# Merging two of three 256-column matmuls of a weight tile into one of 512 columns, and moving sixteen modulation rows

## The chip, the cores and the metric

One NeuronCore of a Trainium2 chip runs the kernel as one program. The metric is the device time of one execution in microseconds, as a median over several runs.

## The reference

Two transformer-like blocks over 256 tokens of width 2048, batch 1, in float32. What matters here is that nearly all of the work is a chain of matrix products with large weights:

```python
mod = (c_act @ ada_w + ada_b)            # 6 x 2048 modulation values
h = rmsnorm(x, norm1_g) * (1 + sc1) + sh1
z = h @ w_in                             # q, k, v, gates, lx, ly, ga, gb
o_a = nsa_attention(...); o_b = gelu(ly) * rg_lru(u, ...)
merged = sigmoid(ga) * (o_a @ proj_a) + sigmoid(gb) * (o_b @ proj_b)
x = x + g1 * (merged @ w_out)
h = rmsnorm(x, norm2_g) * (1 + sc2) + sh2
gate, val = split(h @ w_up)              # 2 x 6144 columns
x = x + g2 * ((gelu(causal_dwconv(gate)) * val) @ w_down)
```

A second block (sliding-window attention, a state-space mixer, a gated output) follows; the change leaves it as it is.

## The kernel before

Activations lie transposed in SBUF: 128 partitions of features by 256 tokens. Each product is made at better than one pass of the reduced float32 type: every weight and every activation is held as a high half (rounded) and a low half (the rest), and a weight tile (128x128 at one k) takes three matmuls with 256 moving columns, high by high, high by low and low by high (`terms` in `unit`, line 1792). Each matmul instruction loads its weights itself. `put_pair` lays the low half of an activation behind its high half, n KB on (n chunks of 128 features).

The products are cut into **groups** of 512 output columns (`groups`, from line 53): kc, vc, k, v, gates, q, lx, ly; then for i from 0 to 3 ga, gb, pa, pb (the sigmoid gates and the two projections); wout 0 to 3; then, once for each half of the feed-forward width, gate and val 0 to 5 in turn and down 0 to 3; then the second block. A group is cut into **units** of two k chunks, eight units for k = 2048 and twelve for down. A unit's weights are one 512 KB load into one of ten slots of a ring (`wraw`). Some slots' loads are followed by a **modulation row**: 128 columns of `ada_w`, a 1 MB load into two slots, which VectorE multiplies by `c` and sums (`ada`, line 1248). `g.ada[s]` says behind which slot of a group a row comes.

For each unit ScalarE rounds the weights to the high half (`split_act`, line 1267; six buffers `whi`, so it waits until TensorE has done the unit six before) and VectorE takes the low half (`split_dve`, line 1272, then the unit's modulation rows). Both run five units ahead of TensorE (`LEAD`). TensorE accumulates a group into a PSUM pair of two banks, `pairs[g % 2]`; four more banks (`bank`, `states_in`) serve the mixers, the norms' sums and the tables.

The order of all engines is written out by hand: every engine walks the same list of units, at each unit does its part of the unit, and then steps the **jobs** that are due (`walk`). A group's evacuation (`evac`) is a job that starts at the first unit of the next group, one step for each unit; a step that hands work to another engine ends there, and the other engine's part comes a unit later. SyncE issues all weight and row loads in slot order. `freed[g % 2]` tells TensorE that the pair may be written again. Two groups, the first half's gate 0 and q2 0, begin behind a flush: the group before is evacuated at once, the norm is computed, and the normalised input is made two chunks per unit (`normed_first`, `normed_rest`, lines 403 to 426).

Evacuations that matter: ga and gb are a ScalarE sigmoid (line 1429), pa and pb VectorE products with it (1452, 1458, 1460), pb 3 also splits the last merged rows (346, 348) and lets POOL reload x into `res` (1468). wout and down add to `res` on VectorE (1488); wout also sums squares in `bank[0]`. gate is a ScalarE scale (1438), a VectorE convolution of three taps (797) and a gelu (1446); val is a VectorE product (1500) and a split (346, 348). Beside the first half's gate 1 to val 3 `ssm_tables` runs on VectorE (lines 945 to 1029), and behind val 3 `make_turns` on POOL.

```python
wh, wl = whi[:, r, :], wlo[:, PLACE[z], :]
terms = lambda k: ((wh, hi[:, k, :]), (wh, lo_at(k)), (wl, hi[:, k, :]))
```

## Time and profile before

| | us |
|---|---|
| median of 3 runs | 2721.61 |
| lowest, highest | 2721.07, 2725.24 |
| the profiled execution | 2722.21 |
| its span, first to last instruction | 2720.5 |

Busy time, the sum over one engine's instructions with overlaps counted once, is given per engine and as a share of the span. PE is TensorE's matmuls and PEld its weight loads, DVE is VectorE, ACT ScalarE, POOL GpSimd; SPq is SyncE's queue, DVEq VectorE's sequencer. Matmuls are pipelined, so the duration of one is longer than the distance between the starts of two; the pace is read from starts. PEclk is the granted clock of TensorE as a share of 2.4 GHz. A line such as L1792 is a line of the kernel. `x` and a number counts instructions. Some matmul records can be missing.

### The profile page before, as it was taken

To read this page: it belongs to the slowest core of one execution; us is meant where nothing else is said; L and a number is where in the kernel's file an instruction comes from. 1 tells how busy PE (TensorE), PEld (TensorE's weight loads), DVE (VectorE), ACT (ScalarE), POOL (GpSimd) and SP (SyncE) were. 2 spreads that over 40 slices of the span, in tenths; PEclk is the share of its full clock that TensorE was granted. 3 is DMA by queue.
4 is the path that set the end of the run, shared out by engine and by line. 5 is a ranking of instruction groups with operands and counts; after the bars stand their busy time and mean duration, and the time that the engine had idled before them with its cause. 6 is when DMAs were issued, how large, how long until landed. Compare 5 with 4: busy or idle time off the path is not lost.

```text
span 2720.5 us, 48148 instructions
## 1 busy us (share of the span) xinstructions
PE 2609.1 (96%) x20256; PEld 2514.8 (92%) x20256; DVE 1883.2 (69%) x2519; ACT 1113.5 (41%) x1381; POOL 229.7 (8%) x190
## 2 busy tenths in 40 slices
PE   7989999999999999899999999999999999999999
PEld 5779989889999999899999999999898888899999
DVE  7865666675866675679985566554486898897563
ACT  1023455454443343454343344444443444534432
POOL 0000000000000000000366530001100000000000
PEclk9988999999999999999999999999999999999999
DMA  9964455455888886478776676665555554465654
GB/s 405 424 245 153 148 185 175 144 178 180 281 271 276 277 269 226 141 238 275 264 226 212 217 219 184 182 185 179 163 180 175 156 161 132 150 188 171 206 178 135
DMA packets 243462, 568.13 MB, mean 209 GB/s; under 512 B 17424, under 2 KB 21520, under 8 KB 228784
## 3 DMA queue, kind: packets, MB, share of 16 engines
q1 hardware_dynamic: 233776, 530.33, 60.2%
q0 software_dynamic: 9472, 34.74, 3.5%
q8 instruction: 160, 2.62, 0.4%
q14 instruction: 54, 0.44, 0.1%
HBM read 550.85 MB, written 14.16 MB: 208 GB/s over the span
## 4 chain that ended last, share of the span: by engine, by line
PE 74%; DVE 12%; DVEq 5%; ACT 4%; DMA 3%; issue 2%; SPq 0%; POOL 0%; ACTq 0%
PE pair L1792 65%; DVE wlo L1272 4%; DMA wraw<-ada_wT_dram 2%; ACT whi L1267 2%; DVE wraw L1248 1%; PE pair L1365 1%; DVEq L338 1%; PE bank L499 1%; PE pair L1798 1%; PE pair L1785 1%; DMA wraw<-w_in_dram 1%; PE states_in L1097 1%; PE bank L1365 1%; PE states_in L1370 1%; PE states_in L684 0%
## 5 line engine op out<-in xcount | busy, mean ns | idle before, releaser
L1272 DVE TENSOR_TENSOR wlo<-wraw,whi 128x1024 fp32r<-128x1024 f32 x777 | 988.3, 1279 | 650.5 <-ACT whi L1267 627.3
L1267 ACT ACTIVATE whi<-wraw 128x1024 fp32r<-128x1024 f32 x777 | 818.0, 1058 | 1328.4 <-PE pair L1792 837.7
L1792 PE MATMUL pair<-h_hi,whi 128*128 128x256 f32 x3936 | 1138.0, 289 | 23.3 <-DVE h_lo L426 8.5
L1792 PE MATMUL pair<-h_lo,whi 128*128 128x256 f32 x3936 | 1122.9, 285 | 0.0
L1792 PE MATMUL pair<-h_hi,wlo 128*128 128x256 f32 x3936 | 1122.1, 285 | 0.0
L1792 PEld LDWEIGHTS pair<-h_hi,whi 128*128 128x128 f32 x3936 | 765.0, 194 | 43.3 <-issue 34.6
L1792 PEld LDWEIGHTS pair<-h_lo,whi 128*128 128x128 f32 x3936 | 765.2, 194 | 0.7
L1792 PEld LDWEIGHTS pair<-h_hi,wlo 128*128 128x128 f32 x3936 | 764.5, 194 | 0.0
L1248 DVE SCALAR_TENSOR_TENSOR wraw<-wraw,cb 128x2048 f32<-128x2048 f32 x96 | 221.2, 2306 | 54.5 <-DMA wraw<-ada_wT_dram 53.0
L1792 PE MATMUL pair<-hid_hi,whi 128*128 128x256 f32 x768 | 218.5, 284 | 0.0
L1792 PE MATMUL pair<-hid_hi,wlo 128*128 128x256 f32 x768 | 217.3, 283 | 0.0
L1792 PE MATMUL pair<-hid_lo,whi 128*128 128x256 f32 x768 | 217.3, 283 | 0.0
L1792 PEld LDWEIGHTS pair<-hid_lo,whi 128*128 128x128 f32 x768 | 147.4, 192 | 0.2
L1792 PEld LDWEIGHTS pair<-hid_hi,whi 128*128 128x128 f32 x768 | 147.4, 192 | 0.2
L1792 PEld LDWEIGHTS pair<-hid_hi,wlo 128*128 128x128 f32 x768 | 147.4, 192 | 0.0
L1792 PE MATMUL pair<-m_hi,whi 128*128 128x256 f32 x512 | 145.5, 284 | 0.0
L1792 PE MATMUL pair<-m_lo,whi 128*128 128x256 f32 x512 | 144.9, 283 | 0.0
L1792 PE MATMUL pair<-m_hi,wlo 128*128 128x256 f32 x512 | 144.9, 283 | 0.0
L1792 PEld LDWEIGHTS pair<-m_lo,whi 128*128 128x128 f32 x512 | 98.3, 192 | 0.1
L1792 PEld LDWEIGHTS pair<-m_hi,whi 128*128 128x128 f32 x512 | 98.3, 192 | 0.1
L1792 PEld LDWEIGHTS pair<-m_hi,wlo 128*128 128x128 f32 x512 | 98.3, 192 | 0.0
L1365 PEld LDWEIGHTS pair<-h_f,wfour 128*128 128x128 f32 x256 | 49.7, 197 | 27.9 <-issue 21.3
(443 smaller groups left out, 3312.4 us busy)
## 6 DMA issues: line engine op xcount, KB each, us to landing
wraw<-w_in_dram SPq DMA_DIRECT2D x312, 512.0 KB, 3.7
wraw<-ada_wT_dram SPq DMA_DIRECT2D x96, 1024.0 KB, 5.7
wraw<-ffn_up_dram SPq DMA_DIRECT2D x192, 512.0 KB, 3.7
wraw<-ffn_down_dram SPq DMA_DIRECT2D x96, 512.0 KB, 4.0
wraw<-w_out_dram SPq DMA_DIRECT2D x64, 512.0 KB, 4.3
wfour<-w_in_dram SPq DMA_DIRECT2D x16, 1024.0 KB, 13.2
wraw<-proj_a_dram SPq DMA_DIRECT2D x32, 512.0 KB, 5.1
wraw<-proj_b_dram SPq DMA_DIRECT2D x32, 512.0 KB, 4.9
```

Source lines behind the costliest of these rows:

```text
L338: return ve.drain() if self.me == "dve" else None
L499: ins = te.matmul(bank[1][:, 0, 0:60], wcmp[which][:, l, :], blocks[:, l, :], start=(l == 0), stop=(l == 31))
L1097: ins = te.matmul(states_in[:, q, c, :], bz[rows, m % 2, c, :], u_2[rows, m, :], start=True, stop=True)
L1248: ve.scalar_tensor_tensor(out=row, in0=row, scalar=1.0, in1=cb[:, :], op0=ALU.mult, op1=ALU.mult, accum_out=mod[:, col:col + 1]).then_inc( ...
L1267: sc.activation(whi[:, r, 0:w], wraw[:, PLACE[z], 0:w], ACT.Copy).then_inc(hi_ready, 1)
L1272: ve.tensor_tensor(wlo[:, PLACE[z], 0:w], wraw[:, PLACE[z], 0:w], whi[:, r, 0:w].bitcast(F32), ALU.subtract).then_inc(lo_ready, 1)
L1365: ins = te.matmul(out, w[:, g * CB + o * P:g * CB + (o + 1) * P], x, start=(c == 0 and o % 2 == 0), stop=(c == DC - 1), skip_group_check=True)
L1370: ins = te.matmul(flat(bank[2 + b][:, :, :]), x[:, b * P:(b + 1) * P], w[:, 3 * CB:4 * CB], start=(c == 0), stop=(c == DC - 1))
L1785: ins = te.matmul(pair[:, 2 * b, 0:48], x[:, b * P:(b + 1) * P], w[:, k * 48:(k + 1) * 48], start=(k == 0 and t == 0), stop=(k == 15 and t ...
L1792: ins = te.matmul(pair[:, o, :], w[:, at_w + o * P:at_w + (o + 1) * P], x, start=(k == 0 and o % 2 == 0 and t == 0), stop=(k == last and t ...
L1798: ins = te.matmul(flat(pair[:, 2 * b:2 * b + 2, :]), x[:, b * P:(b + 1) * P], w[:, at_w:at_w + CB], start=(k == 0 and t == 0), stop=(k == ...
```

## The change

- `groups` marks 41 groups as wide: pb 0 to the first half's down 3 without wout, and the second half's gate 0 to val 5. In these groups the mixers that use the four other banks are at rest.
- PSUM is laid out anew: two blocks of four banks (`wides`). A pair is the first two banks of a block; `bank` and `states_in` are the other two of each. A wide group uses all four banks of its block, one for each 128 output columns.
- `put_pair` also gives one view of both halves, so that one matmul can take the high and the low half of a chunk as 512 moving columns, in two runs of 256. In a wide group a weight tile takes two matmuls: the high weight half by both halves of the input (512 columns), and the low weight half by the high input half (256 columns, added to the first 256).
- `evac` of a wide group first has ScalarE copy the second 256 columns of each bank to `tl`, then VectorE adds the first 256 to it and frees the banks; the rest of the evacuation reads `tl` in place of PSUM. pa and pb now wait for the sigmoid itself where their gate group is wide.
- The sixteen modulation rows 80 to 95, two in each of gate and val 1 to 4, are spread: two in wout 0, one each in wout 1 and 2, and one each in gate and val 0 to 5 of the first half. `ctmp` moves, to make room for `tl`.

```diff
--- before.py
+++ after.py
@@ -48,6 +48,7 @@
         self.units = 1 if mode == "GATES" else 2 * slots
         self.ada = {}
         self.flush = False
+        self.wide = False
 
 
 def groups():
@@ -92,9 +93,15 @@
     at = [(out[of(kind, i)], s) for i in range(4) for kind in ("ga", "gb", "pa", "pb") for s in (1, 3)]
     for n, (g, s) in enumerate(at):
         g.ada[s] = [(64 if n % 2 == 0 else 48) + n // 2]
-    at = [(out[of(kind, i)], s) for i in range(1, 5) for kind in ("gate", "val") for s in (1, 3)]
+    at = [(out[of("wout", i)], s) for i, s in ((0, 1), (0, 3), (1, 1), (2, 1))]
+    at += [(out[of(kind, i)], 2) for i in range(6) for kind in ("gate", "val")]
     for n, (g, s) in enumerate(at):
         g.ada[s] = [80 + n]
+
+    for g in range(of("pb", 0), of("down", 3, 0) + 1):
+        out[g].wide = out[g].kind != "wout"
+    for g in range(of("gate", 0, 1), of("val", 5, 1) + 1):
+        out[g].wide = True
     for kind, i, half in (("gate", 0, 0), ("q2", 0, 0)):
         out[of(kind, i, half)].flush = True
     return out, of
@@ -111,7 +118,8 @@
         return nc.alloc_sbuf_tensor_at(name, list(shape), dt, offset=base + at)
 
     def put_pair(name, at, n):
-        return put(name + "_hi", at, [P, n, T], F32R), put(name + "_lo", at + n * 1024, [P, n, T], F32R)
+        both = put(name, at, [P, 2, n, T], F32R)
+        return both[:, 0, :, :], both[:, 1, :, :], both
 
     K = 1024
 
@@ -214,17 +222,20 @@
     ssp = vector("ssp", [P, 5, 32])
     wgate = put("wgate", off, [P, 2, 4, P])
     b1 = put("b1", off, [P, DC])
-    ctmp = put("ctmp", off, [P, 4, 256])
+    ctmp = put("ctmp", z1 + 28 * K, [P, 4, 256])
+    tl = put("tl", off, [P, 4, T])
     bz = put("bz", off, [P, 2, 2, P])
     xg, yf = put("xg", off + 2 * K, [P, T]), put("yf", off + 3 * K, [P, T])
 
     def V(name, n=0, w=1):
         return vec[:, VEC[name] + n:VEC[name] + n + w]
 
-    pairs = [ctx.enter_context(nc.psum_tensor(f"pair{n}", [P, 4, T], F32)) for n in range(2)]
-    bank = [ctx.enter_context(nc.psum_tensor(f"bank{n}", [P, 2, T], F32)) for n in range(2)]
-    states_in = ctx.enter_context(nc.psum_tensor("states_in", [P, 2, 2, T], F32))
-    bank += [states_in[:, 0], states_in[:, 1]]
+
+
+    wides = [ctx.enter_context(nc.psum_tensor(f"banks{n}", [P, 4, 2, T], F32)) for n in range(2)]
+    pairs = [w[:, 0:2, :, :].rearrange("p b c t -> p (b c) t") for w in wides]
+    bank = [wides[n // 2][:, 2 + n % 2, :, :] for n in range(4)]
+    states_in = wides[1][:, 2:4, :, :]
 
     def sem(name):
         return ctx.enter_context(nc.semaphore(name))
@@ -342,7 +353,7 @@
     flat = lambda t: t.rearrange("p a b -> p (a b)")
 
     def split(dst, at, n, src):
-        hi, lo = dst
+        hi, lo = dst[0], dst[1]
         ve.tensor_copy(hi[:, at:at + n, :], src)
         ve.drain()
         return ve.tensor_tensor(lo[:, at:at + n, :], src, hi[:, at:at + n, :].bitcast(F32), ALU.subtract)
@@ -414,7 +425,7 @@
 
     def normed_low(j, b, name, rounded, dst, shift=None):
         me, ins = j.me, None
-        hi, lo = dst
+        hi, lo = dst[0], dst[1]
         tt = (t1, t2)[b // 2 % 2][:, 2 * (b % 2):2 * (b % 2) + 2, :]
         j.take("act_to_dve", "dve", rounded)
         if me == "dve":
@@ -1409,6 +1420,18 @@
                 "gs2": (ACT.Sigmoid, lambda: (gs_2[:, 4 * i:4 * i + 4, :], e[:, :, :]))}
         rows = lambda t, n=1: t[:, 4 * i:4 * i + 4, :]
 
+        if gr.wide:
+
+            e, w = tl, wides[g % 2]
+            yield from j.hand("to_act", "dve", "act", j.drained())
+            if computed("act"):
+                ins = sc.activation(tl[:, :, :], w[:, :, 1, :], ACT.Copy)
+            yield from j.hand("act_to_dve", "act", "dve", ins)
+            if me == "dve":
+                done(ve.tensor_tensor(tl[:, :, :], w[:, :, 0, :], tl[:, :, :], ALU.add))
+                ve.drain()
+            done = lambda ins: ins
+
         if g in (2, 3):
             if computed("dve"):
                 for b in range(2):
@@ -1426,7 +1449,9 @@
             if computed("act"):
                 f, ends = FUNC[k]
                 dst, src = ends()
-                done(sc.activation(dst, src, f))
+                ins = done(sc.activation(dst, src, f))
+            if gr.wide:
+                j.ready[k] = j.give("act_to_dve", "act", ins)
         elif k in ("lx", "gate"):
             if k == "lx":
                 taps, wname, bname, ci, stride = 4, "lru_conv_w", "lru_conv_b", 4 * i, DC
@@ -1446,13 +1471,17 @@
                     ins = sc.activation(t1[:, :, :], t1[:, :, :], ACT.Gelu_apprx_tanh)
                 j.ready["gelu"] = j.give("act_to_dve", "act", ins)
         elif k == "pa":
-            if me == "dve":
+            if GR[of("ga", i)].wide:
+                j.take("act_to_dve", "dve", j.ready["ga"])
+            elif me == "dve":
                 j.eng.wait_ge(*evacuated("ga", i))
             if computed("dve"):
                 done(ve.tensor_tensor(rows(res), t1[:, :, :], e[:, :, :], ALU.mult))
                 ve.drain()
         elif k == "pb":
-            if me == "dve":
+            if GR[of("gb", i)].wide:
+                j.take("act_to_dve", "dve", j.ready["gb"])
+            elif me == "dve":
                 j.eng.wait_ge(*evacuated("gb", i))
             if computed("dve"):
                 done(ve.tensor_tensor(t2[:, :, :], t2[:, :, :], e[:, :, :], ALU.mult))
@@ -1765,7 +1794,7 @@
         def unit(g, gr, u, n):
             r, z = u % HI, unit_slot[u]
             pair, last = pairs[g % 2], 2 * gr.units - 1
-            hi, lo = X[gr.x]
+            hi, lo = X[gr.x][0], X[gr.x][1]
             lo_at = (lambda k: lo[k // 4][:, k % 4, :]) if gr.x == "ys" else (lambda k: lo[:, k, :])
             if n == 0 and g >= 2:
                 pe.wait_ge(freed[g % 2], g // 2 if g >= 6 else 1)
@@ -1786,7 +1815,14 @@
                                             start=(k == 0 and t == 0), stop=(k == 15 and t == 2))
             for kk in range(0 if gr.mode == "GATES" else 2):
                 k, at_w = 2 * n + kk, kk * CB
-                if "T" in gr.mode:
+                if gr.wide:
+                    for o in range(4):
+                        out, cols = wides[g % 2][:, o, :, :], slice(at_w + o * P, at_w + (o + 1) * P)
+                        te.matmul(out, wh[:, cols], X[gr.x][2][:, :, k, :], start=(k == 0), stop=(k == last),
+                                  skip_group_check=True)
+                        ins = te.matmul(out[:, 0, :], wl[:, cols], hi[:, k, :], start=False, stop=(k == last),
+                                        skip_group_check=True)
+                elif "T" in gr.mode:
                     for o in range(4 if gr.mode == "T" else 2):
                         for t, (w, x) in enumerate(terms(k)):
                             ins = te.matmul(pair[:, o, :], w[:, at_w + o * P:at_w + (o + 1) * P], x,
```

## Rows read from the trace of the kernel before

**Rows 1.** The page: busy time by engine; chain that ended last, by engine.

```profile
PE 2609.1 (96%) x20256; PEld 2514.8 (92%) x20256; DVE 1883.2 (69%) x2519; ACT 1113.5 (41%) x1381; POOL 229.7 (8%) x190
...
PE 74%; DVE 12%; DVEq 5%; ACT 4%; DMA 3%; issue 2%; SPq 0%; POOL 0%; ACTq 0%
```

**Rows 2.** Stretches: from:to, length; busy PE, PEld, DVE, ACT, POOL; clock, DMA.

```profile
700.00:1053.00 353.00, 352.46 (x2936) 352.12 (x2934) 242.57 (x212) 137.79 (x133) 3.21 (x3) 1.00 0.81 274
...
1200.00:1300.00 100.00, 100.00 (x836) 100.00 (x834) 88.24 (x180) 47.36 (x53) 0.00 (x0) 1.00 0.81 275
1300.00:1340.00 40.00, 35.69 (x279) 34.98 (x278) 37.49 (x54) 13.46 (x13) 12.23 (x7) 0.96 0.71 227
1340.00:1870.00 530.00, 530.00 (x4419) 530.00 (x4418) 338.17 (x324) 220.37 (x230) 165.20 (x108) 1.00 0.67 207
```

**Rows 3.** The chain in order of time: start, us, what.

```profile
703.95 348.89 PE pair L1792 x2904
...
1337.43 533.03 PE pair L1792 x4440
```

**Rows 4.** Stretches as in rows 2: the tables, and around the wait.

```profile
1186.00:1324.00 138.00, 137.31 (x1144) 137.11 (x1143) 119.54 (x230) 65.32 (x73) 0.00 (x0) 1.00 0.80 272
1301.00:1351.00 50.00, 45.69 (x363) 44.98 (x362) 46.61 (x59) 19.34 (x21) 20.19 (x12) 0.97 0.74 243
```

**Rows 5.** Waits, PE and DVE, 1140 to 1345: us in total, times, longest.

```profile
PE pair L1792 <- DVE wlo L1272: 4.3, 4, 2.6
...
DVE wraw L1248 <- DMA wraw<-ada_wT_dram: 5.6, 3, 2.3
```

**Rows 6.** Timeline of PE, value group: start, us; eight more starts lie between.

```profile
198.79 0.39 PE L1798 MATMUL pair<-wlo,h_hi 128*128 128x512 f32 x1
...
200.83 0.39 PE L1798 MATMUL pair<-wlo,h_hi 128*128 128x512 f32 x1
```

**Rows 7.** Timeline of PE after the flush; 21 more starts lie between.

```profile
1119.22 0.41 PE L1792 MATMUL pair<-h_lo,whi 128*128 128x256 f32 x1
...
1123.91 0.38 PE L1792 MATMUL pair<-h_hi,wlo 128*128 128x256 f32 x1
```

**Rows 8.** Groups by line, ACT, whole span: busy, mean ns, idle before, releasers.

```profile
L1267 ACT ACTIVATE whi<-wraw 128x1024 fp32r<-128x1024 f32 x776 | 817.2, 1058 | 1322.8 <-PE pair L1792 837.7 <-DMA wraw<-w_in_dram 235.2 <-DMA wraw<-ffn_up_dram 77.6
...
L1429 ACT ACTIVATE t<-pair 128x1024 f32<-128x1024 f32 x12 | 12.3, 1028 | 13.9 <-DVEq L338 13.6
```

**Rows 9.** Groups by line, DVE, 700 to 1420.

```profile
L1272 DVE TENSOR_TENSOR wlo<-wraw,whi 128x1024 fp32r<-128x1024 f32 x246 | 319.4, 1311 | 143.1 <-ACT whi L1267 136.5 <-issue 0.2
L1248 DVE SCALAR_TENSOR_TENSOR wraw<-wraw,cb 128x2048 f32<-128x2048 f32 x44 | 102.4, 2328 | 34.2 <-DMA wraw<-ada_wT_dram 33.8
...
L1500 DVE TENSOR_TENSOR t<-t,pair 128x1024 f32<-128x1024 f32 x6 | 7.3, 1212 | 0.0
```

**Rows 10.** DMA issues: queue, count, KB each, median us from issue to landing.

```profile
res<-xT_dram POOLq DMA_DIRECT2D x1, 2048.0 KB, 14.5
```

**Rows 11.** Timeline of DVE, evacuation of pb 3 and of wout 0.

```profile
1020.35 0.69 DVE L346 CAST m_hi<-res 128x1024 fp32r<-128x1024 f32 x1
1021.11 1.22 DVE L348 TENSOR_TENSOR m_lo<-res,m_hi 128x1024 fp32r<-128x1024 f32 x1
...
1040.78 1.65 DVE L1488 SCALAR_TENSOR_TENSOR res<-pair,mod,res 128x256 f32<-128x256 f32 x4
```

**Rows 12.** Timeline of DVE in gate 0 of the first half.

```profile
1121.51 1.23 DVE L1272 TENSOR_TENSOR wlo<-wraw,whi 128x1024 fp32r<-128x1024 f32 x1 [0.95 <-ACT whi L1267]
...
1142.50 0.87 DVE L426 SCALAR_TENSOR_TENSOR h_lo<-t,mod,h_hi 128x256 fp32r<-128x256 f32 x2
```

**Rows 13.** Timeline of PE in gate 0 of the first half.

```profile
1136.50 0.38 PE L1792 MATMUL pair<-h_hi,whi 128*128 128x256 f32 x1 [0.71 <-DVE h_lo L426]
...
1140.46 0.38 PE L1792 MATMUL pair<-h_hi,whi 128*128 128x256 f32 x1 [0.84 <-DVE h_lo L426]
```

**Rows 14.** Timeline of DVE, POOL at work.

```profile
1324.17 2.13 DVE L1272 TENSOR_TENSOR wlo<-wraw,whi 128x1024 fp32r<-128x1024 f32 x1 [0.18 <-issue]
```

## The prediction

> **What bounds the kernel now.** First the page: TensorE is busy 96% of the span, and 74% of the chain that ended last is its work; VectorE (DVE) has 69% and 12% [rows 1]. Busy times of matmuls overlap, so next the stretches: from 700 to 1053 us and from 1340 to 1870 us matmuls run without a gap at a granted clock of 1.00, while DVE is busy 64 to 69% and ScalarE (ACT) about 40%; only near 1300 does TensorE fall back, with DVE at 94% [rows 2]. The two long pieces of the chain give the pace: 348.89 us for 2904 matmuls and 533.03 us for 4440, 120.1 ns for each 256-column matmul with its own weight load [rows 3]. A wide group can be faster only by what a matmul costs apart from its columns.
>
> One stretch is different. Between 1186 and 1324 us DVE is busy 119.5 of 138 us; besides weight splitting and evacuation it carries the state-space tables and two modulation rows per group [rows 4]. It falls behind until TensorE waits four times, 4.3 us in all [rows 5]. In the 50 us from 1301 on 363 matmuls ran, where the pace of other stretches (836 in 100 us, some 3 of them across the edges) gives 419: 56 x 0.12 = 6.7 us lost, part of it at a clock of 0.97 [rows 2, 4].
>
> **The matmuls.** A weight tile (128x128 at one k) now takes three loads and three 256-column matmuls, 3 x 120.1 = 360.2 ns. After, it takes one matmul of 512 columns and one of 256. The nearest row of the first is the value groups' matmul, of the same type and with its own load: from 198.79 to 200.83 us nine starts, 226.7 ns each [rows 6]. With 226.7 + 120.1 = 346.8 ns a tile saves 13.4 ns. Both widths hold the same fixed cost: twice the columns cost 106.6 ns more, so 13.5 ns of 120.1 and of 226.7 stand beside the columns. At the lower clock the same 256 columns take (1123.91 - 1119.22) / 22 = 213.2 ns, which is 1.2 GHz with nothing added [rows 7], so tiles run there save nothing. I take 13.4 ns.
>
> The Trainium skill's page "TensorE: Matmul & The Clock Gate", section "Back-to-back issue gap", puts the cost beside the columns at about 2.5 ns at full clock; by it the matmuls would save 6.7 us in place of the 36.1 below, and the sum would be near 2712. The rows disagree, with 13.5 ns at both widths.
>
> Wide groups: pb 0; ga, gb, pa, pb 1 to 3; gate and val 0 to 5 of both halves; down 0 to 3 of the first half. That is 37 groups of 16 k x 4 tiles and 4 of 24 x 4: 2752 tiles. In the first half's gate 0 the first seven units (56 tiles) wait for the normalised input anyway (below), which leaves 2696 x 13.4 = **36.1 us** gained.
>
> What no row shows: the moving operand of the 512-column matmul lies in two runs of 1 KB (the high and the low half, 16 or 24 KB apart). Rows bound it by 226.7 ns (one run) and 240.2 ns (each run as dear as a matmul now), so the gain by 36.9 us and 0. A bound below 226.7 I leave out: under 512 columns the load already has twice the time to hide in, and the 13.5 ns are still there. I take one run's price: there is one load and one matmul, and by the rows the fixed cost comes once for such a pair.
>
> **Evacuation.** Each of 41 wide groups adds an ACT copy of 1024 columns out of PSUM, nearest 1.03 us [rows 8], and a DVE add, nearest 1.21 us (a multiply of that shape from PSUM) [rows 9]; what follows comes a unit or two later than before. Cost nothing on TensorE in the matmul-bound stretches: in the whole span ACT stood 837.7 us waiting for TensorE before a high-half rounding [rows 8], and DVE idles a third there [rows 2]. The sums are due only when the group after next needs the banks, a whole group (23 us) later. The cover: there are six high-half buffers, so the low half of unit u can be written once unit u-6 is done, 1.06 + 1.3 us later [rows 8, 9]; five units (14 us) less 2.4 us lie between it and its use. Without that cover the price is 41 x 2.24 = 92 us. The waits of pa's and pb's products for the sigmoids are for values reached a group earlier.
>
> One wait gets longer: pb 3's sum, the split of the merged rows and POOL's reload of x come two units and an add later, 7 us. The reload is queued after the split at 1021.11 + 1.2 us and takes 14.5 us, so it lands near 1037 now and near 1044 then; DVE needs it at 1040.78 [rows 10, 11]. DVE would stand some 3 us, with weight splits queued behind, inside the 12 us of cover: nothing. wout 0 needs the last merged rows at its seventh unit, still some 8 us later: nothing.
>
> **The rows that move.** Sixteen modulation rows (2.33 us each on DVE [rows 9]) leave gate and val 1 to 4; four go to wout 0 to 2, where TensorE is far from waiting; twelve go one each to gate and val 0 to 5. SP's queue issues their 1 MB loads in the new order; half as many per group takes pressure from the ten-slot ring, where DVE waited three times, 5.6 us, for a row [rows 5].
>
> In gate 0 the row comes at a bad place: at the first unit after the flush, behind the split of unit 5 and ahead of the rest of the normalising. From there to 1143 each unit is a loop from DVE to ACT and back, 3.96 us long, with TensorE waiting for it at 1136.50 and 1140.46 [rows 12, 13]. The row goes in whole, with its accumulator read: **2.4 us** lost.
>
> In gate 1 to val 3 DVE loses 6 x 2.33 = 14.0 us and gains 6 x (1.21 + 0.07, the gap that a drain leaves after 1020.35 [rows 11]) = 7.7 us: 6.3 us less. TensorE asks 6 x 64 x 13.4 ns = 5.1 us earlier. DVE so ends 1.2 us less behind, and the 5.6 us wait for rows shrinks. Of the 6.7 us I take **2 us** back; the bounds are 6.7 back and 6 lost (twelve adds at over 2 us with what they push back, if they run beside POOL, as a weight split at 1324.17 does [rows 14]).
>
> **Sum**: 2722.2 us (the profiled execution: span 2720.5 and 1.7 around it) - 36.1 + 2.4 - 2 = 2686.5. That execution lay 0.6 above the median of the runs, so **2686 us**, 1.3% faster.
>
> **Rivals.** (a) *DVE becomes the bound in the first half's gate and val.* For: 94% busy near 1300, splits of 2.1 us beside POOL [rows 2, 14]. Against: fewer rows there. The 2 us back turn into 6 lost: 2694. Chance 0.10.
> (b) *The second run costs a matmul's fixed price*, or the 512 columns are issued as two matmuls, so that the change does not do what it says. For: no operand of two runs is in the trace. Against: one load, and the fixed cost comes once with it. No gain at the matmuls; DVE's relief then meets an unchanged pace, about 5 us back: 2722.2 + 2.4 - 5 - 0.6 = 2719. Chance 0.07.
> (c) *Only a fifth of the fixed cost goes*, because the rest of it moves to the 256-column matmul: 2696 x 2.7 ns = 7.3 us, and 2722.2 - 7.3 + 2.4 - 5 - 0.6 = 2712. Against: the same cost at both widths [rows 3, 6]. Chance 0.03. The section of the Trainium skill named above would give this case.
> (d) *Slower: the operand of two runs is read at less than a column a cycle.* It decides from 240.2 ns per 512-column matmul on; each ns above costs 2.75 us. At half rate, 2 x 213.2 ns as at the lower clock [rows 7], it is 186 x 2.75 = 512 us more, about 3231. Against: each run is 1 KB of neighbouring words, like an operand now. Chance 0.06.
> The Trainium skill's page "Advanced Engine Details and Errata", section "PSUM Cachelines", says that non-contiguous patterns slow matmuls; here the output is one whole bank and only the input has a break, which no run shows yet.
>
> **Numbers.** My forecast has 0.74. A measurement of this kernel can tell about 0.2% (5.4 us) from no change. Faster by more: the forecast, (a) and (c), 0.87; within it: (b), 0.07; slower: (d), 0.06. Low end: 36.9 and 6.7 us gained and gate 0's 2.4 lost or hidden, 2678 to 2680; 2677. High end: (a) with half of its bound more, or a third of a second run's 13.4 ns (12 us), 2698; 2700 leaves about 2 in 10 outside.
>
> **What would show it.** Matmul starts alternating by 227 and 120 ns in the wide stretches, units of 2.78 us in place of 2.88, the stretch from pb 0 to wout 0 some 11 us shorter and the second half's gate and val 10 us. Gate 0 longer by 2 us; waits for DVE's low half near val 3 of at most 5 us. A wide pair of 360 ns or more, or waits for DVE in the pure matmul stretches, would prove me wrong.

## The result, and the profile after

The changed kernel takes 2707.49 us (median of 4 runs, 2703.53 to 2711.3) where the kernel before, in the same comparison, takes 2722.2 (4 runs). The ratio is 0.9944, its 95% interval 0.9927 to 0.9961: faster by 14.7 us, where 36 were forecast. The profiled execution took 2711.3 us (span 2709.6), 10.9 less than that of before.

The page of the changed kernel, busy time by engine and the chain by engine, beside [rows 1]:

```profile
PE 2591.2 (96%) x17504; PEld 2365.6 (87%) x17504; DVE 1933.2 (71%) x2560; ACT 1150.2 (42%) x1422; POOL 227.1 (8%) x190
...
PE 74%; DVE 11%; DVEq 4%; ACT 4%; DMA 3%; issue 3%; SPq 0%; POOL 0%; POOLq 0%; ACTq 0%
```

20256 - 17504 = 2752 matmuls are gone, one for each weight tile of a wide group, as counted in the prediction. The same stretches as in [rows 2]:

```profile
700.00:1053.00 353.00, 349.56 (x2124) 310.03 (x2123) 263.52 (x229) 150.75 (x145) 3.56 (x3) 1.00 0.81 283
1200.00:1300.00 100.00, 100.00 (x568) 86.67 (x567) 85.00 (x176) 50.06 (x58) 0.00 (x0) 1.00 0.72 227
1300.00:1340.00 40.00, 35.90 (x192) 30.27 (x191) 36.39 (x52) 15.97 (x17) 13.48 (x9) 0.96 0.69 223
1340.00:1870.00 530.00, 529.78 (x3161) 467.34 (x3160) 366.81 (x347) 240.64 (x253) 163.84 (x109) 1.00 0.67 209
```

TensorE is still the bound: it is busy without a gap in the second stretch and nearly so in the first and the last. From 1200 to 1300 us there are 568 matmuls, 284 tiles: 352 ns a tile with those at the edges counted in, where the forecast had 346.8.

The timeline of PE in pa 1 (start, us, engine, line), one pair and the pair eight places on:

```profile
799.54 0.40 PE L1821 MATMUL banks<-oa,whi 128*128 128x512 f32 x1
799.78 0.28 PE L1823 MATMUL banks<-oa,wlo 128*128 128x256 f32 x1
...
802.37 0.40 PE L1821 MATMUL banks<-oa,whi 128*128 128x512 f32 x1
802.60 0.28 PE L1823 MATMUL banks<-oa,wlo 128*128 128x256 f32 x1
```

(802.37 - 799.54) / 8 = 353.7 ns a pair; over the 832 pairs from pb 0 to pb 3, 293.97 us from the start of pb 0 to that of wout 0, it is 353.33. The mean distance from a 512-column start to the next is 236.4 ns (226.7 forecast), and from a 256-column start 116.9. A tile so saves 6.7 ns, not 13.4.

Where each group's first matmul starts, in the two profiled executions (us):

| group | before | after | ahead by | since the row above |
|---|---|---|---|---|
| pb 0 | 715.7 | 714.4 | 1.3 | |
| wout 0 | 1015.2 | 1008.4 | 6.9 | forecast +11.1, measured +5.6 |
| gate 0 | 1118.9 | 1115.9 | 2.9 | forecast 0, measured -4.0 |
| val 0 | 1146.4 | 1145.6 | 0.8 | forecast -2.4, measured -2.2 |
| down 0 | 1406.6 | 1400.8 | 5.8 | forecast +9.4 and +2, measured +5.0 |
| second half's gate 0 | 1544.9 | 1537.0 | 7.9 | forecast +5.1, measured +2.1 |
| second half's down 0 | 1821.3 | 1808.3 | 13.0 | forecast +10.3, measured +5.1 |

Every wide group that does not wait gains 0.43 us (64 x 6.7 ns). The rest, 1.3 us gained ahead of pb 0 and 2.1 lost behind the last wide group, lies in groups that stay as they were. Most of it differs from run to run (at pb 0 the other full kernels below stand between 1.2 us behind and 7.4 ahead); yet pa 0, 25.3 us before, takes 1.1 to 2.3 us more in all nine kernels with the new PSUM layout, e4 without wide groups among them. No run shows why.

At wout 0 the chain, in order of time, leaves the matmuls:

```profile
1008.52 5.78 PE banks L1828 x48
1014.36 4.79 DMA wraw<-ada_wT_dram
1019.18 2.29 DVE wraw L1259
1021.48 1.14 DVE tl L1431
1022.77 1.23 DVE t L1487
1024.08 1.23 DVE res L1489
1025.38 0.69 DVE m L357
1026.14 1.22 DVE m L359
1027.42 0.28 issue
1027.71 1.17 POOL res L1497
```

VectorE is at the modulation row of wout 0 and waits for its load; pb 3's sum (L1431), its products and the split of the last merged rows (L359) stand behind it. The split ends at 1027.36, 5 us after its place in [rows 11] (1021.11 + 1.22), although wout 0 began 6.9 us earlier, and TensorE's seventh unit is late (the wait for `m` below). POOL's reload of x goes out at 1027.71, among the weight loads; for one of these ScalarE then waits 11.3 us, and in wout 1 TensorE waits for the norm's sums from POOL. The waits of that stretch (1000 to 1060):

```profile
ACT whi L1278 <- DMA wraw<-w_out_dram: 27.7, 13, 11.3
...
PE banks L384 <- POOLq L378: 1.8, 1, 1.8
PE banks L1828 <- DVE m L359: 1.6, 1, 1.6
```

Near gate 4, beside [rows 5], and the evacuation's two additions, beside [rows 8, 9] (700 to 1420 us):

```profile
PE banks L1821 <- DVE wlo L1283: 4.1, 4, 2.0
```
```profile
L1428 ACT ACTIVATE tl<-banks 128x1024 f32<-128x1024 f32 x25 | 25.7, 1028 | 51.6 <-DVEq L349 51.2
```
```profile
L1431 DVE TENSOR_TENSOR tl<-banks,tl 128x1024 f32<-128x1024 f32 x25 | 30.5, 1218 | 0.1
```

Both additions cost what was forecast (1028 and 1218 ns).

### The profile page after: what moved, and what is told of

Same layout as the page of the kernel before. It is cut to its first block, busy times and chain, and to the rows that moved or that the text cites. A ratio compares the mean times of both kernels' runs of the same rounds, so it can differ in the third digit from the quotient of the medians.

```text
span 2709.6 us, 42837 instructions
## 1 busy us (share of the span) xinstructions
PE 2591.2 (96%) x17504; PEld 2365.6 (87%) x17504; DVE 1933.2 (71%) x2560; ACT 1150.2 (42%) x1422; POOL 227.1 (8%) x190
## 4 chain that ended last, share of the span: by engine, by line
PE 74%; DVE 11%; DVEq 4%; ACT 4%; DMA 3%; issue 3%; SPq 0%; POOL 0%; POOLq 0%; ACTq 0%
PE banks L1828 33%; PE banks L1821 22%; PE banks L1823 11%; DVE wlo L1283 4%; DMA wraw<-ada_wT_dram 3%; ACT whi L1278 2%; PE banks L1376 2%; DVE wraw L1259 1%; DVEq L349 1%; PE banks L510 1%; PE banks L1834 1%; PE banks L1814 1%; PE banks L719 1%; PE banks L1381 1%; PE banks L1108 0%
## 5 line engine op out<-in xcount | busy, mean ns | idle before, releaser
L1828 PE MATMUL banks<-h,whi 128*128 128x256 f32 x4032 | 757.9, 290 | 10.0 <-DVE h L433 8.0
L1821 PE MATMUL banks<-h,whi 128*128 128x512 f32 x1920 | 683.2, 401 | 14.8 <-DVE h L437 10.6
L1828 PEld LDWEIGHTS banks<-h,whi 128*128 128x128 f32 x4032 | 641.0, 195 | 28.9 <-issue 22.9
L1828 PE MATMUL banks<-h,wlo 128*128 128x256 f32 x2016 | 576.1, 286 | 0.0
L1823 PE MATMUL banks<-h,wlo 128*128 128x256 f32 x1920 | 540.6, 282 | 0.0
L1821 PEld LDWEIGHTS banks<-h,whi 128*128 128x128 f32 x1920 | 362.4, 189 | 108.1 <-issue 12.6
L1828 PEld LDWEIGHTS banks<-h,wlo 128*128 128x128 f32 x2016 | 393.0, 195 | 0.0
L1823 PEld LDWEIGHTS banks<-h,wlo 128*128 128x128 f32 x1920 | 364.4, 190 | 0.0
L1828 PE MATMUL banks<-hid,whi 128*128 128x256 f32 x768 | 139.6, 284 | 0.0
L1821 PE MATMUL banks<-hid,whi 128*128 128x512 f32 x384 | 135.8, 399 | 0.2 <-DVE wlo L1283 0.2
L1828 PEld LDWEIGHTS banks<-hid,whi 128*128 128x128 f32 x768 | 119.7, 191 | 0.4
L1828 PE MATMUL banks<-hid,wlo 128*128 128x256 f32 x384 | 108.7, 283 | 0.0
L1823 PE MATMUL banks<-hid,wlo 128*128 128x256 f32 x384 | 107.8, 281 | 0.0
L1376 PE MATMUL banks<-h_f,wfour 128*128 128x256 f32 x384 | 88.5, 388 | 11.9 <-DVEq L1362 11.8
L1828 PE MATMUL banks<-m,whi 128*128 128x256 f32 x512 | 93.0, 284 | 1.6 <-DVE m L359 1.6
L1821 PEld LDWEIGHTS banks<-hid,whi 128*128 128x128 f32 x384 | 72.2, 188 | 18.5 <-issue 0.5
## 6 DMA issues: line engine op xcount, KB each, us to landing
wfour<-w_in_dram SPq DMA_DIRECT2D x16, 1024.0 KB, 13.3
```

What stands on the lines that cost most here:

```text
L1376: ins = te.matmul(out, w[:, g * CB + o * P:g * CB + (o + 1) * P], x, start=(c == 0 and o % 2 == 0), stop=(c == DC - 1), skip_group_check=True)
L1821: te.matmul(out, wh[:, cols], X[gr.x][2][:, :, k, :], start=(k == 0), stop=(k == last), skip_group_check=True)
L1823: ins = te.matmul(out[:, 0, :], wl[:, cols], hi[:, k, :], start=False, stop=(k == last), skip_group_check=True)
L1828: ins = te.matmul(pair[:, o, :], w[:, at_w + o * P:at_w + (o + 1) * P], x, start=(k == 0 and o % 2 == 0 and t == 0), stop=(k == last and t ...
```

## The experiments

The runs of e1 to e4 share 23 runs of the kernel before (median 2721.89, 2713.47 to 2727.31), those of e7 to e9 share 11 (2722.72), and e10 has 7 (2719.65).

**e1: both halves of a chunk side by side**, so that the 512 columns are one run (all but ob).

```diff
-        both = put(name, at, [P, 2, n, T], F32R)
-        return both[:, 0, :, :], both[:, 1, :, :], both
+        if name == "ob":
+            both = put(name, at, [P, 2, n, T], F32R)
+            return both[:, 0, :, :], both[:, 1, :, :], lambda k: both[:, :, k, :]
+        both = put(name, at, [P, n, 2, T], F32R)
+        return both[:, :, 0, :], both[:, :, 1, :], lambda k: both[:, k, :, :]
...
-                        te.matmul(out, wh[:, cols], X[gr.x][2][:, :, k, :], start=(k == 0), stop=(k == last),
+                        te.matmul(out, wh[:, cols], X[gr.x][2](k), start=(k == 0), stop=(k == last),
```

> The changed kernel with the high and the low half of each chunk laid side by side in SBUF (all inputs but ob's), so that the 512 moving columns are one run. Theory A (the break between the two runs costs the missing 6.7 ns a tile): a 512-column and a 256-column matmul together take 347 ns in place of 353.3 where the layout changed, pb's groups stay at 353; 36 groups of 64 tiles and 4 of 96 at 6.7 ns are 18 us less, about 2690 us. Theory B (the cost comes from alternating 512 and 256 columns into one bank): the pair stays at 353 and the time at 2707 us.

Measured: 2708.6 us (6 runs), ratio 0.9949 (0.9932 to 0.9966), no better than the change. But the profiled execution, the fastest of the six, took 2698.59, and its pace is of two kinds. Stretches (from:to, length; PE busy and count; clock, DMA):

```profile
1150.00:1250.00 100.00, 100.00 (x568) 1.00 0.72 228
1450.00:1550.00 100.00, 100.00 (x579) 1.00 0.71 226
```

In the first the pairs take 353.3 ns, although their operand (h2) is one run there; in the second half of the feed-forward the same operand takes 346.7. The pace turns over at one point, inside down 0:

```profile
1400.31 0.40 PE L1824 MATMUL banks<-hid,whi 128*128 128x512 f32 x1
...
1403.49 0.40 PE L1824 MATMUL banks<-hid,whi 128*128 128x512 f32 x1
1403.73 0.28 PE L1826 MATMUL banks<-hid,wlo 128*128 128x256 f32 x1
1404.08 0.47 PE L1824 MATMUL banks<-hid,whi 128*128 128x512 f32 x1
1404.38 0.28 PE L1826 MATMUL banks<-hid,wlo 128*128 128x256 f32 x1
1404.50 0.40 PE L1824 MATMUL banks<-hid,whi 128*128 128x512 f32 x1
...
1407.62 0.39 PE L1824 MATMUL banks<-hid,whi 128*128 128x512 f32 x1
```

Nine pairs take 3.18 us ahead of 1403.49 (353.3 ns each). At 1403.73, the end of a unit, TensorE waits a little (0.35 us to the next start), and from 1404.50 on nine pairs take 3.12 us (346.7 each), and so on to 1797. So the break in the operand does not make the difference, and a new theory was needed: a stream of pairs has two paces, and each restart after a wait picks one. The time came out as theory B had it, but B has no place for the fast pace.

**e2: the widths sorted**, four 512-column matmuls of a k, then the four of 256.

```diff
+                    for o in range(4):
+                        out, cols = wides[g % 2][:, o, :, :], slice(at_w + o * P, at_w + (o + 1) * P)
                         ins = te.matmul(out[:, 0, :], wl[:, cols], hi[:, k, :], start=False, stop=(k == last),
```

> The changed kernel with the matmuls of a chunk in another order: the four of 512 columns first, then the four of 256; operands and layout as in the changed kernel. Theory A (the break between two runs costs): nothing changes, 8 matmuls take 4 x 353 = 1413 ns, 2707 us. Theory B (alternating widths, or adding at once to a bank just written, costs): 4 x 347 = 1387 ns, some 18 us less, about 2690 us.

Measured: 2704.85 us (6 runs), ratio 0.9945 (0.9926 to 0.9965). In all wide stretches eight matmuls take 1403.3 ns (16.7 over 4 x 346.7), 0.59 us gained a group: neither theory's 1413 or 1387, but between the two paces, and the same after every wait. The order of widths matters.

**e3: the rows back at their places of before**, the rest as changed; **e4: the rows spread, no group wide.**

```diff
-    at = [(out[of("wout", i)], s) for i, s in ((0, 1), (0, 3), (1, 1), (2, 1))]
-    at += [(out[of(kind, i)], 2) for i in range(6) for kind in ("gate", "val")]
+    at = [(out[of(kind, i)], s) for i in range(1, 5) for kind in ("gate", "val") for s in (1, 3)]
```
```diff
-    for g in range(of("pb", 0), of("down", 3, 0) + 1):
-        out[g].wide = out[g].kind != "wout"
-    for g in range(of("gate", 0, 1), of("val", 5, 1) + 1):
-        out[g].wide = True
```

> The changed kernel with the sixteen modulation rows back in gate and val 1 to 4, two each. Theory R (the moved rows cost 2.2 us in gate 0 and about 4 us in wout 0 and 1, and they pay for VectorE's sums near val 3): those 6 us come back, but VectorE now has 6 x 1.3 us more than before in the tables' stretch and TensorE asks 2.5 us earlier, so the wait near gate 4 grows from about 4 to 14 us or more; about 2711 us. Rival (VectorE has room for the sums anyway): 2701 us, with waits near gate 4 as before.

> The rows moved as in the change, but no group wide (three matmuls a tile, evacuation as before; the new PSUM layout stays). Theory R: gate 0 loses 2.2 us and the 6.7 us lost near gate 4 come back whole, since VectorE has less to do there; wout 0 and 1 lose up to 4 us if the row loads alone delay the weights, nothing if it takes pb 3's longer evacuation as well. So 2718 us (only gate 0 pays) or 2722 us (wout pays too).

Measured: e3 2722.06 us (10 runs), ratio 0.9999 (0.9987 to 1.0011); e4 2717.81 (10 runs), ratio 0.9989 (0.9977 to 1.0000). Waits of PE from 1140 to 1410, of e3:

```profile
PE banks L1820 <- DVE wlo L1282: 19.8, 11, 4.5
```

In e3 TensorE waits 19.8 us for low halves between gate 1 and val 5: from val 0's start to down 0's it loses 13.3 us on before, where the changed kernel gains 5.0. That eats all that its wide groups gain elsewhere, and both expectations are missed (by 11 and 21 us): the waits are those of theory R, only larger. wout 0 to gate 0, with no row there, lose nothing (0.00 us a group). In e4 the waits near gate 4 are gone whole, 6.7 us gained on val 4's start, against 2.4 lost at wout 1 and 2.2 at gate 0; wout 0, with its two rows, loses nothing there. So e4's 2718 us, expected where gate 0 alone pays, came out by luck: wout 1 paid too, and the interval reaches up to no change. The split of the last merged rows, in e3 and then in e4:

```profile
1022.27 1.22 DVE L358 TENSOR_TENSOR m<-res,m 128x1024 fp32r<-128x1024 f32 x1
```
```profile
1022.62 1.23 DVE L355 TENSOR_TENSOR m<-res,m 128x1024 fp32r<-128x1024 f32 x1
```

wout 0 starts at 1009.26 and at 1011.79, so the split ends 14.2 us after that with the wide evacuation alone and 12.1 with the rows alone, against 7.1 before and 19.0 with both, in the change (1027.36 - 1008.36). At the pace of before (2.88 us a unit) the seventh unit is due at 17.3: only both together are late.

In e3 (its operands in two runs, as in the change) the pairs run at 346.7 ns from 1137.8 to 1229.0 and from 1343.0 to 1367.9, at 353.3 from pb 0 to pb 3 and from 1377 to 1820, and the pace turns over only at waits.

**e5: the pace by itself.** Nine orders, eight restarts each (ahead of restart r VectorE copies 16 + 30 r columns), 24 tiles a run, all operands constant.

```python
for s, (kind, r) in enumerate(RUNS):
    pe.wait_ge(go, s + 1)
    last = None
    for n in range(TILES):
        last = kind(n) or last
```

> This kernel computes nothing of the reference: TensorE alone runs nine orders of matmuls of constant data, each eight times, with a short wait for VectorE (of eight lengths) ahead of each run of 24 tiles. Theory (phase): a stream of 512- and 256-column matmuls in turn has two paces, 346.7 and 353.3 ns a pair; the restart after a wait picks one, and it then holds until the next wait. So pairs of two-run and of one-run operands each show both paces among their eight restarts, every run of 24 tiles shows one pace throughout (8.32 or 8.48 us for 24 pairs), and 512 columns by themselves take 226.7 ns with one run and with two. Rival (operand): two runs cost 6.7 ns: 512 columns from two runs take 233.3 ns by themselves, pairs of one run 346.7 ns and pairs of two runs 353.3 ns after every restart. Rival (order): what goes first decides, so that 256-first pairs, or pairs entered from a stream of 256 columns without a wait, have one pace in all eight restarts. In twos and fours of a width the phase theory gives 16.7 ns over the ideal for eight matmuls in fours, as seen before, and says nothing for twos (between 0 and 27 ns per eight).

Measured. The first row is 24 matmuls of 512 columns in one run each, the second 24 of two runs:

```profile
180.88 5.73 PE L54 MATMUL banks<-close,whi 128*128 128x512 f32 x24 [0.30 <-DVEq L136]
...
229.59 5.74 PE L58 MATMUL banks<-apart,whi 128*128 128x512 f32 x24 [0.30 <-DVEq L136]
```

Both settle at 226.7 ns: two runs cost nothing. Pairs of two-run operands, first and second restart, first and last start of 24 pairs:

```profile
278.30 0.50 PE L62 MATMUL banks<-apart,whi 128*128 128x512 f32 x1 [0.29 <-DVEq L136]
...
286.76 0.28 PE L63 MATMUL banks<-apart,wlo 128*128 128x256 f32 x1
287.35 0.49 PE L62 MATMUL banks<-apart,whi 128*128 128x512 f32 x1 [0.31 <-DVEq L136]
...
295.66 0.28 PE L63 MATMUL banks<-apart,wlo 128*128 128x256 f32 x1
```

8.46 and 8.31 us for the same instructions: 353.3 and 346.7 ns a pair in the steady part. The faster pace came after 2 of 8 restarts with two runs, 3 of 8 with one run, 3 of 8 with the 256 columns first, and after none of 8 where the pairs followed 256-column matmuls with no wait. Phase holds; operand and order rivals fall, but for the last case, which is that of pb 0 in the kernel. In twos (512, 512, 256, 256) a tile took 348.3 ns after all eight restarts.

**e6: more orders.** A is 512 columns, B 256; every second restart goes through 24 to 27 matmuls of 256 columns.

```python
for c in order * (TILES * 2 // len(order)):
    out, cols, k = at(tile[c])
    tile[c] += 1
    ...
```

> This kernel computes nothing of the reference: TensorE alone again, 24 weight tiles a run with two-run operands, in eight orders of the 512-column (A) and 256-column (B) matmuls, each after eight restarts; every second restart is followed by 24 to 27 matmuls of 256 columns with no wait ahead of the order. Ideal for 24 tiles: 24 x (226.7 + 120.0) = 8320 ns. Phase theory: AB in turn has two paces (8320 or 8480 ns, and the slow one whenever it is entered from 256 columns without a wait), while an order that holds two of one width in a row (AABB anywhere in its period) loses its memory there, so each such order takes the same time after all restarts: AABB 8360 ns, the mixed ones between 8320 and 8480, and the longer its stretches of AB the nearer to one of the two. Rival (chance): the paces have nothing to do with the order, and the mixed orders too come out at two or more times from restart to restart. An order that takes under 8360 ns after all eight restarts would be the one to use in the kernel.

Measured: AB again at two paces (one of four plain restarts fast, all four behind 256 columns slow); AABB 348.3 ns a tile after all eight. Of the others ABABAABB took 351.6, AABABABB 353, AABABABABABABABB about 352, AAABBB 350 and eights about 349. ABABABABABABAABB took 347.0 in the second eight of its tiles after seven of eight restarts, but 352 in the first eight; over all 24 tiles no order beat AABB after every restart. First and last starts of 24 tiles, AB after a wait, then AABB:

```profile
127.87 0.50 PE L52 MATMUL banks<-apart,whi 128*128 128x512 f32 x1 [0.32 <-DVEq L88]
...
136.33 0.28 PE L54 MATMUL banks<-apart,wlo 128*128 128x256 f32 x1
...
191.82 0.50 PE L52 MATMUL banks<-apart,whi 128*128 128x512 f32 x1 [0.29 <-DVEq L88]
...
200.05 0.40 PE L54 MATMUL banks<-apart,wlo 128*128 128x256 f32 x2
```

That each order has one time holds for the short ones; those with long AB stretches still differ a little with the restart.

**e7: AABB in the kernel.**

```diff
-                        ins = te.matmul(out[:, 0, :], wl[:, cols], hi[:, k, :], start=False, stop=(k == last),
-                                        skip_group_check=True)
+                        if o % 2:
+                            for o2 in (o - 1, o):
+                                out, cols = wides[g % 2][:, o2, :, :], slice(at_w + o2 * P, at_w + (o2 + 1) * P)
+                                ins = te.matmul(out[:, 0, :], wl[:, cols], hi[:, k, :], start=False, stop=(k == last),
+                                                skip_group_check=True)
```

> The changed kernel with its matmuls in the order AABB (two weight tiles' 512-column matmuls, then their two 256-column ones) in place of ABAB; nothing else differs. Phase theory: 348.3 ns a tile after every restart in place of 353.3, in all wide groups (0.75 us gained on a group before the change in place of 0.43; down 1.13 in place of 0.64), so 2700 tiles x 5.0 ns = 13.5 us less than the changed kernel: 2694 us, or up to 2697 where TensorE, now earlier, waits longer for VectorE near the first half's gate 4. Rival (the bench does not carry over, since in the kernel other engines use the memories): groups as in the changed kernel, 2707.

Measured: 2698.47 us (6 runs), ratio 0.9913 (0.9895 to 0.9931), 9.0 us under the changed kernel where 13.5 was expected. Every wide group that does not wait gains 0.75 us, and down 1 to 3 1.12 each, as expected. Of the 4.5 us that are short, 1.6 lie at wout 0 and 1 (5.6 lost, 4.0 in the change); the rest is within the spread of the runs (2692.97 to 2701.56). One stretch, beside the 568 of the change:

```profile
1600.00:1700.00 100.00, 100.00 (x576) 1.00 0.66 190
```

**e8 to e10: the rows elsewhere**, all with AABB.

The two lines of the diff that place the rows become, in e8, e9 and e10:

```python
    at = [(out[of("wout", i)], 1) for i in (1, 2, 3)] + [(out[of("val", 0)], 2)]
    at += [(out[of(kind, i)], 2) for i in range(1, 5) for kind in ("gate", "val")]
    at += [(out[of(kind, 5)], s) for kind in ("gate", "val") for s in (1, 3)]
```
```python
    at = [(out[of("wout", i)], s) for i in (2, 3) for s in (1, 3)] + [(out[of("val", 0)], 2)]
    at += [(out[of("gate", i)], 2) for i in (1, 2, 3)] + [(out[of("gate", 4)], s) for s in (2, 3)]
    at += [(out[of(kind, i)], s) for kind, i in (("val", 4), ("gate", 5), ("val", 5)) for s in (1, 3)]
```
```python
    at = [(out[of("wout", i)], s) for i, s in ((1, 1), (2, 1), (2, 3), (3, 1), (3, 3))] + [(out[of("val", 0)], 2)]
    at += [(out[of(kind, i)], 2) for i in range(1, 6) for kind in ("gate", "val")]
```

> As e7_twos, and the modulation rows of gate 0, val 0's neighbours and wout 0 moved: wout 1, 2 and 3 one each, val 0 one, gate and val 1 to 4 one each, gate and val 5 two each. Theory (the rows at gate 0 and wout 0 are where the change loses): gate 0 gets back 2.2 us, and wout 0 and 1 some 1.9 to 3.9 us: 2688 to 2690. Rival (pb 3's longer evacuation and the later reload of x cost wout 0 its time, and not the row): only gate 0's 2.2 us come back, 2692.

> As e7_twos, and the modulation rows kept away from VectorE's full stretch too: wout 2 and 3 two each, val 0 one, gate 1, 2 and 3 one each, none in val 1 to 3, gate 4, val 4, gate 5 and val 5 two each. Theory (VectorE's rows there make TensorE's waits near gate 4): five rows of 2.33 us fewer between gate 1 and val 3 than in e8, so the waits for a low half near gate 4 (4.1 us in the changed kernel's profile) go, and with gate 0 and wout 0 as in e8: 2684 to 2686. Rival (the waits come from the tables' work and POOL's contention alone): waits of 4 us or more stay, 2688 to 2690.

Measured: e8 2695.93 us (5 runs), ratio 0.9900 (0.9878 to 0.9921), e9 2702.65 (6 runs), 0.9930 (0.9910 to 0.9951): both above what was expected, e9 by 17 us. In both, wout 0 to 3 and gate 0 lose 0.0 us: with the sum, the split and the reload of pb 3 as in the change, and no row at wout 0. So pb 3's longer evacuation by itself costs nothing; by e4 the rows by themselves cost nothing at wout 0 either, but 2.4 us at wout 1. But two rows in each of the last gates and vals bring new waits. Waits of PE, e8 from 1380 to 1420, then e9 from 1200 to 1420:

```profile
PE banks L1822 <- DVE wlo L1284: 5.3, 1, 5.3
```
```profile
PE banks L1822 <- DVE wlo L1284: 16.3, 6, 5.8
```

In e8 it is one wait, in down 0, on a low half that stands behind the last row and gate 5's convolution in VectorE's order:

```profile
1384.79 2.28 DVE L1260 SCALAR_TENSOR_TENSOR wraw<-wraw,cb 128x2048 f32<-128x2048 f32 x1
...
1393.00 7.04 DVE L809 SCALAR_TENSOR_TENSOR t<-tl,vec,t 128x255 f32<-128x255 f32 x8
1400.16 1.23 DVE L1284 TENSOR_TENSOR wlo<-wraw,whi 128x1024 fp32r<-128x1024 f32 x1
```

e9 has such waits at gate 4, gate 5 and down 0, 4.1 to 6.1 us to the next start. So the tables alone do not make them (e4 has them too, without such a wait). Nor do two rows a group: before, gate and val 1 to 3 had two each and lost nothing. What is new at gate 5 and down 0 is the convolution's own length. In e8 with POOL idle, then in e4, which reads PSUM there and not `tl` in SBUF, with POOL at work:

```profile
1342.89 3.40 DVE L809 SCALAR_TENSOR_TENSOR t<-tl,vec,t 128x255 f32<-128x255 f32 x8
```
```profile
1340.79 3.38 DVE L804 SCALAR_TENSOR_TENSOR t<-banks,vec,t 128x255 f32<-128x255 f32 x8
1339.80 2.23 POOL L955 TENSOR_TENSOR turned<-px,py 128x512 f32<-128x512 f32 x1 [0.24 <-issue]
1342.18 1.06 POOL L957 TENSOR_TENSOR px<-ph 128x512 f32<-128x512 f32 x1
```

From `tl` beside POOL's turns it takes 7.04 us in e8, 8.58 and 7.06 in e9, 7.08 in the change (down 0): 3.6 to 5.2 us more, of waits of 4.8 to 5.8 at gate 5 and down 0. So most of each of these waits is the convolution, whose source the wide evacuation moved from PSUM to SBUF; how much of the rest is the rows' is not shown. With one row a group the slow convolution cost the change 0.4 us. At e9's gate 4 (3.8 us) no convolution stands ahead, but a row and splits of low halves that are longer beside POOL as well, 3.4 and 2.1 us.

> As e7_twos, with the modulation rows where e7, e8 and e9 lost nothing to them: wout 1 one, wout 2 and 3 two each, val 0 one, gate and val 1 to 5 one each; none in wout 0 and gate 0, and never two in a group behind a gate. Theory: e7's losses at wout 0 and 1 (5.6 us) and at gate 0 (2.1 us) are the rows' and go, nothing new comes at gate 5 or down 0 (e8 and e9 lost 7 and 14 us there with two rows a group): 2698.5 - 7.7 = 2691 us. Rival (any row near the end of the first half's gate and val costs what it costs): 2695 or more.

Measured: 2691.59 us (4 runs, 2688.76 to 2693.54), ratio 0.9901 (0.9877 to 0.9925), the time that was expected. wout 0 to gate 0 lose 0.0; near gate 4 and down 0 TensorE still waits 7.0 us, 1.9 of them at down 0 behind a convolution of 8.63 us:

```profile
PE banks L1821 <- DVE wlo L1283: 7.0, 5, 2.0
```

Its median is the lowest of all, but its runs of before were faster too, and by the ratio it can't be told from e8 (0.9900). In the profiled executions, from pb 0 to the second half's down 0, it gains 29.3 us on before, e8 22.9, e7 22.6 and the change 11.7.

## Why the prediction was wrong

**The step that failed: the matmuls' term, "With 226.7 + 120.1 = 346.8 ns a tile saves 13.4 ns".** Both of its halves were right one by one: the 512-column matmul from two runs does take 226.7 ns, with its fixed 13.5 ns once (e5), and a stream of pairs can take 346.7 ns (e1, e3, e5). What no row of before showed, and what the step took for granted, is that two widths in turn cost the sum of what each costs alone. They do only at one of two paces. The changed kernel's profile shows the other, 6.7 ns more a pair, in nearly all of its wide stretches. Mis-sized: 36.1 us forecast, 18.1 (2696 x 6.7) there. The prediction's sign of being wrong, a pair of 360 ns or more, stood too far off to catch it.

**The range** put the 512 columns between 226.7 and 240.2 ns, which holds what was measured (353.3 - 120.0 = 233.3), but its high end took only a third of that price; a half, with wout's loss, lies outside.

**The rivals.** (b) and (d) laid the price to the second run; e5 shows none, so the doubt that the page "Advanced Engine Details and Errata" of the Trainium skill (section "PSUM Cachelines") raised, that non-contiguous patterns slow matmuls, is not borne out for this input. (c) named the nearest time, 2712, but by another way: it wanted the fixed cost at 2.5 ns, as the Trainium skill's page "TensorE: Matmul & The Clock Gate" has it for the gap of a single matmul in isolation (section "Back-to-back issue gap"), and by e5 a 512-column matmul by itself keeps 226.7 - 2 x 106.6 = 13.5 (106.6 as worked out from [rows 3, 6]). (a) came in part: e3 shows VectorE as the bound with the old rows (19.8 us of waits); with the new ones it is 4.1.

**Evacuation at nothing**: right where POOL rests. Thirteen groups from pb 0 to pb 3 gain 0.43 us each with both additions running; no wait on them is seen there. Not foreseen was that the convolution, now read from `tl`, takes 7.1 us in place of 3.4 beside POOL; in the change that cost 0.4 us at down 0.

**"four go to wout 0 to 2, where TensorE is far from waiting"**, and **pb 3's longer evacuation at nothing**: wrong together, 4.0 us. Each was priced by itself. The 7 us later that the prediction gave to pb 3's split are right (7.1 in e3), but they leave 3 us until wout 0's seventh unit (17.3 - 14.2), not "some 8 us", and the row's 5.0 (12.1 - 7.1 in e4) do not fit into that: 1.9 us lost at wout 0. The other 2.1, at wout 1, are the rows' own (2.4 in e4). TensorE was not waiting there, but the loads had little room: a DMA share of 0.81 up to 1053 us in [rows 2], and POOL's 2 MB reload comes there too. wout 0's two rows are 2 MB more. The step costed VectorE's 2.33 us and not the queue.

**Gate 0's row**: right, 2.4 forecast, 2.2 lost, with the row between the split and the normalising as told.

**The relief near gate 4, 2 us**: val 0 to down 0 gained 5.0 us where the pace alone gives 11 x 0.43 = 4.7, so 0.3, with 0.4 lost again at down 0's start. Its two sides are far larger than their sum: e4 has all 6.7 back from the rows, the prediction's upper bound, while e3 loses 13 with the additions and no rows moved.

**The sum, again**: 18.1 - 4.0 - 2.2 - 0.1 = 11.8 us; the table's wide parts give 13.0 - 1.3 = 11.7.

## What to carry to other kernels

When two sizes of matmul are mixed in one stream, measure the mix: the sum of what each takes alone can be missed by a fixed amount at every turn, and the order AABB avoided most of it here (348.3 ns a tile, where the sum is 346.7). Work that is moved into a stretch where the bound engine does not wait must be priced in all queues that it passes, its loads above all. Two delays that each fit into the same slack need not both fit: take them off it one after the other. Before an engine is given more work beside a bound stretch, look where its longest single pieces stand in its order, and what a new source of their operands does to their length: one row a group was free in most places, two ahead of a convolution that POOL slows cost 5 us or more.

## What the runs showed of the hardware

A stream of 512- and 256-column matmuls in turn, each with its own weight load, at a granted clock of 1.00, has two exact paces, 346.67 and 353.33 ns a pair (at 2.4 GHz 832 and 848 cycles). Which one holds is settled when TensorE starts again after a wait, and it then held for as much as 1256 pairs without a change. Behind a stream of 256 columns without a wait it was the slow one in all 12 cases by itself and at pb 0 in all three kernels with that order (the change, e1, e3). What picks it after a wait stays open: the same eight pauses gave 2, 3 and 3 fast starts. The order AABB took 348.3 ns a tile in all 16 runs by itself and in the kernel.

Eight convolution steps of VectorE (128x255) took 3.4 us with all operands in SBUF and POOL idle, 7.0 to 8.6 with POOL at work beside them (the change, e3, e8, e9, e10), and 3.4 beside POOL where one operand came from PSUM (e4). What the two engines share there no run shows.
